# Gated feed-forward layers on one core: the down projection's pieces dealt among the products of each unit of seven

## The chip, the core and the metric

The kernel runs on one core of a Trainium2 chip. The metric is the device time of one execution in microseconds (us). TensorE does the matrix products, VectorE (DVE) most of the additions and subtractions, ScalarE (ACT) the roundings and copies, GpSimd (POOL) the sums of weights, and SyncE (SP) issues the transfers from the chip's memory. Each engine works through a queue of its own in the order in which the program was written, and waits at a semaphore where an operand is not yet made or a buffer not yet free.

## The reference

Two transformer blocks run one after the other on 512 tokens of width 1024. All weights and activations are float32. What matters here is the feed-forward part:

```
# first block, one layer
x = x + square(relu(rmsnorm(x, g) @ w_ff1)) @ w_ff2            # 1024 -> 4096 -> 1024

# second block, layers i = 0, 1
h = rms_norm(x, ffn_norm[i])
g = einsum('bsd,df->bsf', h, w_gate[i])                        # 1024 -> 2816
u = einsum('bsd,df->bsf', h, w_up[i])
x = x + einsum('bsf,fd->bsd', silu(g) * u, w_down[i])          # 2816 -> 1024
```

Three kinds of attention and their projections stand around it; the change does not touch them.

## The kernel before

Every float32 number is used as a rounded high part and the low part that is left over. A product of two such numbers takes three matmuls: high by high, high by low and low by high. In the trace a high part is `hh`, `wh` or `sums_high`, a low part `hl`, `wl` or `sums_low`; a low part is the subtraction at L2147, on DVE. Where a low part is written over its source the trace shows it under that name.

The kernel has three stages of feed-forward layers: stage 0 is the first block's (relu squared), stages 1 and 2 are the two gated layers of the second block. Most of their up and gate columns are computed in *units of seven* (class `Seven`): a product of 2 by 2 blocks with seven block products in place of eight. A unit of a gated stage yields two tiles of 128 features by 512 tokens, either of the gate or of the up matrix. The units alternate, gate, up, gate, up, sixteen in each gated stage. This is what one unit asks of each engine:

- **PE**: seven products P0 to P6, each of 12 matmuls of 128 columns by 256 tokens in three groups of four (L1343 high by high, L1346 with the tokens' low part, L1349 with the weights' low part).
- **DVE**: the low parts of the weights' seven operands (`wo_lo`, below lo0 to lo6, L2147), the additions that combine the products (`wc`, L2388, L2392 and L2397), and for the finished tiles a multiplication (`wf`, L2411: gate times sigmoid, or gate times up) and, for an up unit, the low part of the product that goes to the down projection (`wf_lo`, L2147, `R<-W,R`).
- **ACT**: the high parts of the operands, copies out of PSUM (L1897 and its neighbours), the sigmoid, and the high part of the finished tile (`wf_hi`, L1905).
- **POOL**: four sums of weights S1, S2, S4, S3 of the unit after the next (`ws`, L2769, four additions one behind the other).
- **SP**: the transfer of the weights of the unit after the next (`wq`, L2996). SP waits for the last low part (lo6) of a unit before it issues it, because the transfer lands in that unit's buffer.

Behind each unit of seven stands a *down unit*: 256 of the rows of `w_down` that belong to features finished earlier, or other rows of the same kind. It has four pieces d0 to d3, each of six matmuls 128 by 512 (L1265 twice, L1268 twice, L1271 twice), and each piece of it that ends is added to the residual `x` on DVE (L2438). The weights of the down units go through two buffers (raw, wh, wl): ACT rounds the high part (L1731), DVE makes the low part (`wl`, L2147), and a buffer is free when the last piece that reads it is done.

What sets the order of all this is the function `dense`. It makes a list of units and their pieces, moves some of them, and then goes through it: behind each piece it puts the steps for the other engines that the piece releases, and the steps that were put off (`defer`: so many pieces later). Each engine's queue is this list, cut to its own steps. The two lines that move pieces are L421 and L422 to L423; the second of them swaps P6 with the piece behind it, so that a unit runs P0 to P5, d0, P6, d1, d2, d3. `seven` names the steps of one product, with the distances of the final tiles' steps at L486 and L488 to L492. `preparation` puts the steps ahead of a stage at positions counted in pieces (sums of tokens `t_sum`, `t_hi`, `t_lo`, the first sums of weights `ws`), and `gated` inside `make` hands them to `dense`.

Of the kernel before, what the change touches and what calls it, by code (L numbers as in the profile page):

```python
# [196 lines left out]
SUMS_USED = (2, 0, 1, 3)  # L197
# [114 lines left out]
class Plan:  # L312
# [92 lines left out]
    def dense(self, units, more=None, crossed=False, hold=0, behind=False):  # L405

        n, order, held = 0, [], []  # L410
        for u in units:
            if u.kind == "win":
                pieces = [(k, 0, 0) for k in range(7)]
            elif u.kind == "rows":
                pieces = [(0, j * u.nk + k, j * u.nk + k + 2) for j in range(u.n) for k in range(0, u.nk, 2)]
            else:
                pieces = [(i, a, a + 2) for i in range(4) for a in range(0, 8, 2)]
            order += [(u, piece) for piece in pieces]
        if crossed:
            order = order[:3] + order[4:6] + order[3:4] + order[6:]  # L420
        for i in range(len(order) - 1, 0, -1):  # L421
            if order[i - 1][0].kind == "win" and order[i - 1][1][0] == 6:  # L422
                order[i - 1], order[i] = order[i], order[i - 1]  # L423
        for i, (u, piece) in enumerate(order):
            tick, extra = self.due() if behind else self.low() + self.due(), (more or {}).get(n, [])
            if behind:
                for step in self.low():
                    self.defer(1, *step)
            after = order[i + 1][0] if i + 1 < len(order) else u
            n += 1  # L430
            if u.kind == "win":
                yield [("wp", u, piece[0])], self.seven(u, piece[0]) + tick + extra
                continue
            self.place(u)
            if u.kind == "rows" and piece[2] % u.nk == 0:
                steps = self.ready(u, piece[2] // u.nk - 1)
                if u.ev == "out" and after.kind == "win" and after.stage and steps[0][0] == "split":
                    self.defer(2, *steps.pop(0))
                    self.defer(4, *self.lows.pop())
                if n <= hold:  # L440
                    held.append(steps.pop())
                    tick += steps + extra
                else:
                    self.gated(u)
                    tick += steps[:-1] + extra + steps[-1:]
            else:
                tick += extra
            if held and n > hold:
                tick.append(held.pop(0))
                self.gated(tick[-1][1])  # L450
            if u.halved(piece[1] // u.nk) and piece[2] % u.nk:
                tick += [("ev_half", u), ("ship_half", u)]
            if u.kind == "cols" and piece[2] == 8:
                if piece[0] == 3:
                    tick.append(("ev", u))
                    if u.ev == "dq":
                        self.heads(u)
                tick += self.split(u.chunks[piece[0]] + 2)
            yield [("mm", u, *piece)], tick
        rest = self.due(True)  # L460
        if rest:
            yield [], rest

    def seven(self, u, k):

        first, i = [], u.product(k)
        if k == 2:
            first.append(("wc", u, 1))
        if k == 5:
            first.append(("wcp", u, 3))  # L470
            self.defer(1, "wc", u, 2)
        if k in (1, 4):
            first.append(("wcp", u, {1: 1, 4: 2}[k]))
        if i + 3 < 7 * (u.last + 1):
            first.append(("wo_hi", i + 3))
        if i + 2 < 7 * (u.last + 1):
            first.append(("wo_lo", i + 2))
        if k == 6 and u.v + 2 <= u.last:
            first += [("wq", self.wins[u.v + 2]), ("ws", self.wins[u.v + 2])]
        if k == 6:  # L480
            self.defer(1, "wc", u, 3)
            if u.ev == "gate":
                self.defer(1, "wsig", u, 0)
                self.defer(2, "wsig", u, 1)
                self.defer(3, "wf", u, 0)
                self.defer(6, "wf", u, 1)  # L486
            else:
                late = u.stage and u.v < u.last  # L488
                for t in range(2):
                    self.defer((1, 6 if late else 2)[t], "wf", u, t)  # L490
                    self.defer((1, 7 if late else 2)[t], "wf_hi", u, t)
                    self.defer((2, 8 if late else 3)[t], "wf_lo", u, t)  # L492
        return first

    def preparation(self, v, stage, wins, tick):

        more, w = {}, wins[0].v
        last_up = self.last_up[stage]

        def put(n, *step):  # L500
            more.setdefault(n, []).append(step)

        put(tick + 3, "wq", wins[0])
        plain = stage == 0
        end = 32 if plain else 48
        for m in range(8):
            put(((13, 14, 16, 17, 18, 20, 21, 22) if plain else (14, 15, 17, 18, 20, 21, 23, 24))[m], "hn", v, stage, m)
        put(14, "ws", wins[0])
        for k in range(4):
            put(((22, 24, 25, 27) if plain else (26, 28, 30, 32))[k], "t_sum", stage, k)  # L510
            put(((24, 25, 27, 28) if plain else (28, 29, 31, 33))[k], "t_hi", stage, k)
            put(((28, 38, 49, 51) if plain else (34, 39, 57, 59))[k], "t_lo", stage, SUMS_USED[k])
        put(29, "wo_hi", 7 * w)
        put(31, "wo_lo", 7 * w)
        put(30, "wo_hi", 7 * w + 1)
        put(end + 10 if plain else end - 1, "wo_lo", 7 * w + 1)
        for i in range(3):
            put(end + i, "b_hi", stage, i, last_up)
            put(end + 2 + i, "b_lo", stage, i)
        put(end + (9 if plain else 10), "wq", wins[1])  # L520
        put(end + (9 if plain else 10), "ws", wins[1])
        put(end + 3, "wo_hi", 7 * w + 2)
        return more
# [2397 lines left out]
def sync_program(sp, S, B, plan, dram):  # L2921
# [65 lines left out]
    def seven(u):  # L2987
# [5 lines left out]
        else:  # L2993
# [3 lines left out]
            S[f"wq{u.v % 2}"], 16)  # L2997

    todo = {"wq": seven, "begin": begin, "split": split, "late": late, "c_turn": c_turn, "c_kt": c_kt, "again": again, "ship": ship, "ship_half": ship_half}
    for step in plan.steps:  # L3000
        if step[0] in todo:
# [85 lines left out]
```

## Time and profile before

| what | value |
|---|---|
| median of 3 runs | 2108.47 us (2108.09 to 2110.71) |
| the profiled execution's own time | 2110.2 us |
| its span in the trace | 2108.4 us |
| PE busy | 2092.7 us, 99% of the span |
| DVE busy | 1468.1 us, 70% |
| ACT busy | 1054.8 us, 50% |
| POOL busy | 407.6 us, 19% |
| granted clock of TensorE | 1.0 (the higher of its levels, 2.4 GHz) |
| the sixteen units of stage 1 | 1231.4 to 1476.3 us |
| the sixteen units of stage 2 | 1832.5 to 2079.6 us |

The span is what the trace covers, first instruction to last; the execution's own time is 1.8 us more. All times in the rows below are counted from the span's start. PE counts as busy from the start of a matmul to its modelled end, so neighbouring matmuls overlap: where PE runs without a break, the pace is the distance from start to start.

### The profile page before, as it was taken

The page shows a single profiled execution, that of the slowest core. Times are in us where ns is not written, and L with a number is a line of the kernel's source. Part 1 is how long each engine was busy: PE and PEld are TensorE (multiplying, and loading weights), DVE is VectorE, ACT ScalarE, POOL GpSimd, SP SyncE. Part 2 cuts the span into 40 slices and gives each one's busy share as a digit, 9 for nine tenths or more (in the row PEclk, how much of TensorE's full clock was granted, in tenths as well). Part 3 has the DMA queues.
Part 4 walks back from the last instruction along what each step waited for, and adds up shares of the span by engine and source line. Part 5 has one row for each costly group of instructions (what it writes and reads, how often), then busy time and mean ns, then how long its engine had stood idle before and what let it go on. Part 6 is the DMA issues. An engine that isn't in the chain of part 4 may idle for free.

```text
span 2108.4 us, 31641 instructions
## 1 busy us (share of the span) xinstructions
PE 2092.7 (99%) x12528; PEld 1731.9 (82%) x12528; DVE 1468.1 (70%) x2153; ACT 1054.8 (50%) x1798; POOL 407.6 (19%) x350
## 2 busy tenths in 40 slices
PE   9999999999999999999999999999999999999999
PEld 7768778778889898887777889999877667899998
DVE  5584774564587777664667888777657678888775
ACT  4463544554354343444455556555445565556553
POOL 0000432102012323010110133343011101143340
PEclk9999999999999999999999999999999999999999
DMA  4212112123242222122111332322221113232322
GB/s 173 80 61 84 58 55 95 48 64 129 90 140 87 114 91 110 62 95 84 51 61 62 118 111 91 121 91 90 80 90 60 60 41 110 91 120 91 119 102 70
DMA packets 45938, 187.18 MB, mean 89 GB/s; under 512 B 5216, under 2 KB 5728, under 8 KB 40032
## 3 DMA queue, kind: packets, MB, share of 16 engines
q1 hardware_dynamic: 45648, 184.98, 25.5%
q8 instruction: 100, 1.64, 0.3%
q14 instruction: 46, 0.38, 0.1%
q10 hardware_dynamic: 144, 0.18, 0.0%
HBM read 183.05 MB, written 2.10 MB: 88 GB/s over the span
## 4 chain that ended last, share of the span: by engine, by line
PE 93%; DVE 4%; ACT 1%; issue 1%; DMA 0%; SPq 0%; DVEq 0%; ACTq 0%
PE ps L1265 17%; PE ps L1268 16%; PE ps L1271 16%; PE ps L1346 7%; PE ps L1349 7%; PE ps L1343 7%; PE ps L1289 4%; PE ps L1292 4%; PE ps L1290 4%; PE ps L1244 3%; PE ps L1399 1%; PE ps L1451 1%; PE ps L1672 1%; PE ps L1654 1%; PE ps L1423 1%; PE ps L1469 1%
## 5 line engine op out<-in xcount | busy, mean ns | idle before, releaser
L1731 ACT CAST wh<-raw 128x1024 fp32r<-128x1024 f32 (+1 forms) x246 | 257.7, 1048 | 330.0 <-PE ps L1271 245.5
L2769 POOL TENSOR_TENSOR Q<-Q 128x512 f32<-128x512 f32 x176 | 268.8, 1527 | 775.3 <-DMA Q<-in_sevens 764.8
L2147 DVE TENSOR_TENSOR wl<-raw,wh 128x1024 fp32r<-128x1024 f32 (+2 forms) x250 | 308.4, 1234 | 151.8 <-ACT wh L1731 151.4
L1265 PE MATMUL ps<-R,wh 128*128 128x512 f32 x892 | 286.4, 402 | 0.2 <-DVE W L2326 0.2
L1268 PE MATMUL ps<-R,wl 128*128 128x512 f32 x892 | 276.9, 391 | 0.5 <-DVE wl L2147 0.5
L1271 PE MATMUL ps<-R,wh 128*128 128x512 f32 x892 | 276.1, 390 | 0.0
L1265 PE MATMUL ps<-hh,wh 128*128 128x512 f32 x704 | 231.2, 409 | 2.1 <-ACT wh L1737 0.9
L1268 PE MATMUL ps<-hh,wl 128*128 128x512 f32 x704 | 218.4, 391 | 0.6 <-DVE wl L2147 0.6
L1271 PE MATMUL ps<-hl,wh 128*128 128x512 f32 x704 | 217.5, 390 | 0.0
L1268 PEld LDWEIGHTS ps<-R,wl 128*128 128x128 f32 x892 | 167.2, 188 | 37.6 <-DVE wl L2147 1.4
L1271 PEld LDWEIGHTS ps<-R,wh 128*128 128x128 f32 x892 | 167.5, 188 | 36.1
L1265 PEld LDWEIGHTS ps<-R,wh 128*128 128x128 f32 x892 | 157.9, 189 | 35.2 <-issue 9.7
L2438 DVE TENSOR_TENSOR x<-ps,x 128x512 f32<-128x512 f32 x191 | 130.7, 688 | 77.9 <-PE ps L1271 75.3
L1265 PEld LDWEIGHTS ps<-hh,wh 128*128 128x128 f32 x704 | 125.4, 188 | 39.2 <-issue 15.1
L1268 PEld LDWEIGHTS ps<-hh,wl 128*128 128x128 f32 x704 | 131.8, 188 | 30.4 <-DVE wl L2147 2.1
L1271 PEld LDWEIGHTS ps<-hl,wh 128*128 128x128 f32 x704 | 132.2, 188 | 29.1 <-DVE hl L2228 0.3
L1289 PE MATMUL ps<-wh,hh 128*128 128x512 f32 (+1 forms) x384 | 155.0, 404 | 0.7 <-DVE F L2296 0.5
L2147 DVE TENSOR_TENSOR hl<-Q,hh 128x512 fp32r<-128x512 f32 (+1 forms) x163 | 143.5, 888 | 8.1 <-ACT hh L1857 8.1
L1292 PE MATMUL ps<-wh,hl 128*128 128x512 f32 (+1 forms) x384 | 148.7, 387 | 0.0
L1290 PE MATMUL ps<-wl,hh 128*128 128x512 f32 (+1 forms) x384 | 148.6, 387 | 0.0
L2147 DVE TENSOR_TENSOR wx<-Q,wx 128x512 fp32r<-128x512 f32 x154 | 132.9, 870 | 9.3 <-ACT wx L1857 9.3
L1905 ACT CAST R<-W 128x512 fp32r<-128x512 f32 x56 | 34.8, 622 | 151.7 <-DVE W L2403 81.9
(281 smaller groups left out, 3676.2 us busy)
## 6 DMA issues: line engine op xcount, KB each, us to landing
raw<-in_weights SPq DMA_DIRECT2D x244, 512.0 KB, 3.5
Q<-in_sevens SPq DMA_DIRECT2D x44, 1024.0 KB, 4.8
x<-in_x_t SPq DMA_DIRECT2D x4, 512.0 KB, 7.0
F<-in_x_t SPq DMA_DIRECT2D x4, 512.0 KB, 4.9
out<-x SPq DMA_DIRECT2D x7, 256.0 KB, 2.0
raw<-in_weights SPq DMA_DIRECT2D x4, 416.0 KB, 3.1
x<-in_bias SPq DMA_DIRECT2D x1, 1024.0 KB, 6.8
F<-in_weights SPq DMA_DIRECT2D x2, 384.0 KB, 3.8
```

Of the source, the lines that this page charges most:

```text
L1265: pe.matmul(out, hi[:, k, cs], B.tile(u.src, k)[0], start=k == 0, stop=False)
L1268: pe.matmul(out, lo[:, k, cs], B.tile(u.src, k)[0], start=False, stop=False)
L1271: last = pe.matmul(out, hi[:, k, cs], B.tile(u.src, k)[1], start=False, stop=k == u.nk - 1)
L1289: pe.matmul(out, B.hh[:, ts], hi[:, kk, :], start=k == 0, stop=False)
L1290: pe.matmul(out, B.hh[:, ts], lo[:, kk, :], start=False, stop=False)
L1292: last = pe.matmul(out, B.hl[:, ts], hi[:, kk, :], start=False, stop=k == 7)
L1343: pe.matmul(out, hi[:, n, :], high[:, n, :], start=n == 0 and k not in (4, 5, 6), stop=False, skip_group_check=True)
L1346: pe.matmul(out, hi[:, n, :], low[:, n, :], start=False, stop=False, skip_group_check=True)
L1349: last = pe.matmul(out, lo[:, n, :], high[:, n, :], start=False, stop=n == 3, skip_group_check=True)
L1731: act.copy(B.wh[s][:, 0:nk * ncol], B.raw[s][:, 0:nk * ncol]).then_inc(S["w_hi"], 1)
L2147: dve.tensor_tensor(lo, src, hi.bitcast(F32), ALU.subtract).then_inc(S[name], 1)
L2769: pool.tensor_tensor(B.weight_part(u.v, out), B.weight_part(u.v, a), B.weight_part(u.v, b), op).then_inc(S["w_s"], 1)
```

## The change

In the two gated stages the four pieces of the down unit are dealt among the products of the unit of seven ahead of it: P0, P1, d0, P2, P3, d1, P4, P5, d2, P6, d3. The swap of P6 and d0 is kept for stage 0 alone. The distances, in pieces, of the steps for the finished tiles are changed with it: the gate's second `wf` comes 5 pieces behind P6 in place of 6, and the up unit's second tile (`wf`, high part, low part) 2, 3 and 4 behind in place of 6, 7 and 8. In `preparation` the first sums of weights of a gated stage are put at position 42 in place of 14, and the last low part of the token sums at 58 in place of 59.

```diff
@@ dense
         if crossed:
             order = order[:3] + order[4:6] + order[3:4] + order[6:]
+        for i, (u, piece) in enumerate(order):
+            if u.kind == "win" and u.stage and piece[0] == 0:
+                order[i:i + 11] = [order[i + n] for n in (0, 1, 7, 2, 3, 8, 4, 5, 9, 6, 10)]
         for i in range(len(order) - 1, 0, -1):
-            if order[i - 1][0].kind == "win" and order[i - 1][1][0] == 6:
+            if order[i - 1][0].kind == "win" and order[i - 1][0].stage == 0 and order[i - 1][1][0] == 6:
                 order[i - 1], order[i] = order[i], order[i - 1]
@@ seven
-                self.defer(6, "wf", u, 1)
+                self.defer(5, "wf", u, 1)
             else:
                 late = u.stage and u.v < u.last
                 for t in range(2):
-                    self.defer((1, 6 if late else 2)[t], "wf", u, t)
-                    self.defer((1, 7 if late else 2)[t], "wf_hi", u, t)
-                    self.defer((2, 8 if late else 3)[t], "wf_lo", u, t)
+                    self.defer((1, 2)[t], "wf", u, t)
+                    self.defer((1, 3 if late else 2)[t], "wf_hi", u, t)
+                    self.defer((2, 4 if late else 3)[t], "wf_lo", u, t)
@@ preparation
-        put(14, "ws", wins[0])
+        put(14 if plain else 42, "ws", wins[0])
-            put(((28, 38, 49, 51) if plain else (34, 39, 57, 59))[k], "t_lo", stage, SUMS_USED[k])
+            put(((28, 38, 49, 51) if plain else (34, 39, 57, 58))[k], "t_lo", stage, SUMS_USED[k])
```

Three lines are added, so a line of the old kernel from L421 on stands three lines lower in the new one (L2147 is L2150 there). The queues of POOL and of SP are the same in both programs, instruction by instruction and wait by wait; those of PE, DVE and ACT differ.

On PE, in the first unit of seven of stage 1 (a gate unit), products are the rows with 128x256 and the down unit's pieces those with `R2` (the high tile), `R3` (its low part) and 128x512. Before, from the fifth product to the second piece:

```order
L1343 MATMUL ps<-sums_high,wx 128x256 x4
L1346 MATMUL ps<-sums_low,wx 128x256 x4
L1349 MATMUL ps<-sums_high,wx 128x256 x4
L1343 MATMUL ps<-hh,wx 128x256 x4
L1346 MATMUL ps<-hl,wx 128x256 x4
L1349 MATMUL ps<-hh,wx 128x256 x4
L1265 MATMUL ps<-R2,wh0 128x512 x2
L1268 MATMUL ps<-R2,wl0 128x512 x2
L1271 MATMUL ps<-R3,wh0 128x512 x2
L1343 MATMUL ps<-sums_high,hh 128x256 x4
L1346 MATMUL ps<-sums_low,hh 128x256 x4
L1349 MATMUL ps<-sums_high,hl 128x256 x4
```

After, in the same unit, from the fourth product to the third piece:

```order
L1346 MATMUL ps<-sums_high,hh 128x256 x4
L1349 MATMUL ps<-sums_low,hh 128x256 x4
L1352 MATMUL ps<-sums_high,hl 128x256 x4
L1268 MATMUL ps<-R2,wh0 128x512 x2
L1271 MATMUL ps<-R2,wl0 128x512 x2
L1274 MATMUL ps<-R3,wh0 128x512 x2
L1346 MATMUL ps<-sums_high,wx 128x256 x4
L1349 MATMUL ps<-sums_low,wx 128x256 x4
L1352 MATMUL ps<-sums_high,wx 128x256 x4
L1346 MATMUL ps<-hh,wx 128x256 x4
L1349 MATMUL ps<-hl,wx 128x256 x4
L1352 MATMUL ps<-hh,wx 128x256 x4
```

A piece stands now between each second product, and only one, d3, is left behind P6 where three were.

On DVE, where the first up unit of stage 1 ends and a gate unit begins: `W3<-ps,W3` is the last combination of the up unit, `W2` and `W3` its two tiles, `R1<-W2,R0` and `R1<-W3,R0` their low parts for the down projection, `hl<-Q0,hh` low parts of the next unit's weights (the first two here are lo2 and lo3), `W4<-ps,W4` the next unit's first combination, `x<-ps,x` a finished piece. Before:

```order
L2397 TENSOR_TENSOR W3<-ps,W3 128x512
L2411 TENSOR_TENSOR W2<-W2,W0 128x512
L2438 TENSOR_TENSOR x<-ps,x 128x512
L2147 TENSOR_TENSOR R1<-W2,R0 128x512
L2438 TENSOR_TENSOR x<-ps,x 128x512
L2147 TENSOR_TENSOR hl<-Q0,hh 128x4x128 x2
L2388 TENSOR_TENSOR W4<-ps,W4 128x256
L2147 TENSOR_TENSOR wx<-Q0,wx 128x512
L2411 TENSOR_TENSOR W3<-W3,W1 128x512
```

After:

```order
L2400 TENSOR_TENSOR W3<-ps,W3 128x512
L2414 TENSOR_TENSOR W2<-W2,W0 128x512
L2441 TENSOR_TENSOR x<-ps,x 128x512
L2150 TENSOR_TENSOR hl<-Q0,hh 128x4x128
L2150 TENSOR_TENSOR R1<-W2,R0 128x512
L2414 TENSOR_TENSOR W3<-W3,W1 128x512
L2150 TENSOR_TENSOR hl<-Q0,hh 128x4x128
L2150 TENSOR_TENSOR R1<-W3,R0 128x512
L2391 TENSOR_TENSOR W4<-ps,W4 128x256
```

Between the piece `x<-ps,x` and the second `hl` (lo3) stand now the first `hl`, a low part of a tile and a multiplication, where the two `hl` stood side by side before.

On DVE at the end of stage 1, behind the last unit of seven: `W6` and `W7` are its two tiles, `R3` their low parts, `wl1` the low part of the down weights for the second unit from there. Before:

```order
L2397 TENSOR_TENSOR W7<-ps,W7 128x512
L2411 TENSOR_TENSOR W6<-W6,W4 128x512
L2438 TENSOR_TENSOR x<-ps,x 128x512
L2147 TENSOR_TENSOR R3<-W6,R2 128x512
L2411 TENSOR_TENSOR W7<-W7,W5 128x512
L2147 TENSOR_TENSOR R3<-W7,R2 128x512
L2438 TENSOR_TENSOR x<-ps,x 128x512
L2147 TENSOR_TENSOR wl1<-raw1,wh1 128x1024
```

After:

```order
L2400 TENSOR_TENSOR W7<-ps,W7 128x512
L2414 TENSOR_TENSOR W6<-W6,W4 128x512
L2441 TENSOR_TENSOR x<-ps,x 128x512
L2150 TENSOR_TENSOR wl1<-raw1,wh1 128x1024
L2150 TENSOR_TENSOR R3<-W6,R2 128x512
L2414 TENSOR_TENSOR W7<-W7,W5 128x512
L2150 TENSOR_TENSOR R3<-W7,R2 128x512
```

The low part `wl1` of the down weights has moved ahead of the second tile's multiplication, which it stood behind.

## Rows read from the trace of the kernel before

**Rows 1.** The page: busy time by engine, and the load of one set of weights.

```profile
PE 2092.7 (99%) x12528; PEld 1731.9 (82%) x12528; DVE 1468.1 (70%) x2153; ACT 1054.8 (50%) x1798; POOL 407.6 (19%) x350
...
L1268 PEld LDWEIGHTS ps<-R,wl 128*128 128x128 f32 x892 | 167.2, 188 | 37.6 <-DVE wl L2147 1.4
```

**Rows 2.** Waits by line, 1800 to 2106 us: total us, times, longest; PE and PEld.

```profile
PE ps L1346 <- DVE sums_low L2147: 1.3, 1, 1.3
...
PEld ps L1343 <- ACT W L1897: 0.3, 1, 0.3
```

**Rows 3.** Windows, units of stages 1 and 2: us; busy PE, PEld, DVE, ACT, POOL; clock.

```profile
1231.40:1476.30 244.90, 244.90 (x1712) 229.87 (x1711) 190.86 (x253) 135.04 (x234) 98.40 (x68) 1.00 0.28 102
1832.50:2079.60 247.10, 245.71 (x1712) 230.07 (x1712) 196.21 (x252) 134.96 (x234) 89.16 (x60) 1.00 0.27 101
```

**Rows 4.** Timeline, PE, one up unit of stage 1: start, duration, engine, line, tiles.

```profile
1340.40 0.64 PE L1343 MATMUL ps<-hh,wx 128*128 128x256 f32 x4
...
1349.03 0.63 PE L1265 MATMUL ps<-R,wh 128*128 128x512 f32 x2
...
1350.42 0.64 PE L1343 MATMUL ps<-sums_high,hh 128*128 128x256 f32 x4
...
1351.85 0.63 PE L1265 MATMUL ps<-R,wh 128*128 128x512 f32 x2
...
1355.96 0.64 PE L1343 MATMUL ps<-hh,wx 128*128 128x256 f32 x4
```

**Rows 5.** Timeline, first unit of stage 2: DVE, POOL and PE.

```profile
1835.00 1.22 DVE L2147 TENSOR_TENSOR sums_low<-sums,sums_high 128x1024 fp32r<-128x1024 f32 x1
1842.09 2.30 DVE L2147 TENSOR_TENSOR sums_low<-sums,sums_high 128x1024 fp32r<-128x1024 f32 x1
...
1836.38 1.30 POOL L2769 TENSOR_TENSOR Q<-Q 128x512 f32<-128x512 f32 x1 [54.80 <-DMA Q<-in_sevens]
...
1844.44 0.74 PE L1346 MATMUL ps<-sums_low,hh 128*128 128x256 f32 x4 [1.25 <-DVE sums_low L2147]
```

**Rows 6.** Timeline, end of stage 1: PE, DVE and ACT.

```profile
1476.33 0.63 PE L1265 MATMUL ps<-R,wh 128*128 128x512 f32 x2
...
1480.43 0.62 PE L1265 MATMUL ps<-R,wh 128*128 128x512 f32 x2
...
1476.53 0.69 DVE L2397 TENSOR_TENSOR W<-ps,W 128x512 f32<-128x512 f32 x1 [2.33 <-PE ps L1349]
...
1479.12 0.69 DVE L2411 TENSOR_TENSOR W<-W 128x512 f32<-128x512 f32 x1
...
1481.72 1.23 DVE L2147 TENSOR_TENSOR wl<-raw,wh 128x1024 fp32r<-128x1024 f32 x1
...
1479.84 0.62 ACT L1905 CAST R<-W 128x512 fp32r<-128x512 f32 x1 [1.37 <-DVE W L2411]
1480.63 1.06 ACT L1731 CAST wh<-raw 128x1024 fp32r<-128x1024 f32 x1 [0.17 <-PE ps L1271]
```

**Rows 7.** Windows, the time behind stage 1; columns as in rows 3.

```profile
1476.30:1600.00 123.70, 123.70 (x567) 98.24 (x566) 71.13 (x105) 56.65 (x98) 10.95 (x12) 1.00 0.26 81
```

**Rows 8.** Timeline, behind the up unit of rows 4: two DVE subtractions beside POOL's sums.

```profile
1356.76 1.35 DVE L2147 TENSOR_TENSOR hl<-Q,hh 128x512 fp32r<-128x512 f32 x1
1358.04 1.78 DVE L2147 TENSOR_TENSOR hl<-Q,hh 128x512 fp32r<-128x512 f32 x1
...
1356.27 1.29 POOL L2769 TENSOR_TENSOR Q<-Q 128x512 f32<-128x512 f32 x1
1357.64 1.63 POOL L2769 TENSOR_TENSOR Q<-Q 128x512 f32<-128x512 f32 x1
```

**Rows 9.** Timeline, from a unit's last low part to POOL's next sums: DVE, SP's queue, POOL.

```profile
1363.01 0.68 DVE L2147 TENSOR_TENSOR hl<-Q,hh 128x512 fp32r<-128x512 f32 x1
...
1363.72 0.33 SPq L2996 DMA_DIRECT2D Q<-in_sevens  x1
...
1368.78 1.30 POOL L2769 TENSOR_TENSOR Q<-Q 128x512 f32<-128x512 f32 x1 [9.51 <-DMA Q<-in_sevens]
```

## Prediction

> **What bounds the kernel now.** I read the page first, then PE's waits, then the two gated stages as windows, and last the timeline at the places that the change touches. The page shows PE busy for 99% of the span [rows 1]: time can be won only where PE waits or runs slower than its matmuls need, and each new wait of PE is lost in full. The window of stage 1 is filled by PE to the last hundredth, 244.90 of 244.90 us. Stage 2 runs the same 1712 matmuls and takes 247.10 [rows 3]; the list of waits names what makes the difference: one wait of 1.3 us on the low part of a token sum and one of 0.3 us on a copy of ACT's [rows 2]. More than these 2.2 us the change cannot take away inside the units, since the granted clock is 1.00 throughout [rows 3]. Whether it brings new waits depends on two reserves: how late DVE finishes a low part before PE wants it, and how many down pieces lie between the last product of a unit and the next reader of its tiles.
>
> **The change part by part.** All times below are measured from starts of matmuls.
>
> *Border between products and pieces.* Six products take 1349.03 − 1340.40 = 8.63 us, the lone piece behind them 1350.42 − 1349.03 = 1.39, the lone product 1351.85 − 1350.42 = 1.43, and the three pieces 1355.96 − 1351.85 = 4.11 [rows 4]. So a run of n products costs 1.44n − 0.01, a run of n pieces 1.36n + 0.03: each pair of runs carries 0.02 us. A unit has two pairs of runs before and four after. 32 units × 2 × 0.02 = +1.3 us; bounds 0 and 2.6.
>
> The Trainium skill, page "TensorE: Matmul & The Clock Gate", section "Back-to-back issue gap", lets the distance between matmuls depend on their columns alone. By that rule the sum would be 1.3 us smaller; the lone piece at 1.39 us against 1.36 in a run speaks against it.
>
> *Waits that go.* In the first unit of stage 2, P6 waits for the second low part of the token sums. It stands before at 1842.09, behind subtractions that POOL's sums slow down from 1836.38 on; in the new order it follows directly on the one at 1835.00, ahead of POOL's start [rows 5]. PE then wants it eight us after it is made. This gives back at least the 1.3 + 0.3 of [rows 2] and at most the 2.2 of [rows 3], which holds the restarts too: −1.9 us. Earlier final tiles (distances 5 and 2, 3, 4) take nothing from PE's own queue.
>
> *First sums of weights at position 42.* POOL's queue and its waits are the same in both programs, and `ws` is a step of POOL alone. What starts these sums is the transfer, not the place in the list. Cost 0, with no other end to bound.
>
> *End of each gated stage.* Let P6 of the last unit end at 0 (1476.33). Before, three pieces follow, and the final down unit starts at 4.10 (1480.43) [rows 6]; its first piece reads tiles made earlier, its second one, 1.37 later at 5.47, the two of the last unit. After, only d3 follows: the final unit starts at 1.39, its second piece at 2.76, and the second matmul of that, 1.37/6 = 0.23 on, reads the second tile's high part at 2.99. When is that made? By the rows: combination at 0.20 (1476.53), then the first tile's multiplication. In the new order DVE then takes the finished piece (d3 is seen at 1.39 + 0.20 = 1.59) and, next, wl1. That waits for ACT's wh1, which in its turn waits for d3, the last reader of its buffer, as it did before (1480.63, 0.20 behind 1480.43). So wh1 runs from 1.59 to 2.65, wl1 starts at 2.68 and lets the next operation in after 1.23 − 0.08 = 1.15, at 3.83. Then the first tile's low part for 0.61, then the multiplication of the second tile, 4.44 to 5.13, then ACT's rounding 0.03 later for 0.62, to 5.78, and 0.05 to PE (the step from DVE's end at 1844.39 to PE's start at 1844.44 in [rows 5]): 5.83. PE waits 5.83 − 2.99 = 2.84 us; the first groups after a wait ran 0.74 in place of 0.64 [rows 4, 5], some 0.1 to 0.2 in all: 3.0. Before, that multiplication (1479.12) stood ahead of wl1 (1481.72) and the rounded tile was there at 1480.46, 4.13, with 1.3 us to spare. Two stages: +6.0 us, bounds 5.2 and 6.6.
>
> *From an up unit to the gate unit behind it.* There are seven such places in each stage, 14 in all. POOL makes its four sums when the transfer has landed; SP issues that when lo6 of the unit is done, and from lo6's end (1363.69) to POOL's start (1368.78) it took 5.09 us [rows 9]. Before, lo6 ended 1363.69 − 1355.96 = 7.73 into the unit, so POOL starts 2.74 us ahead of the next unit. After, lo6 stands behind the addition of the second piece d1, which ends at 2 × (2 × 1.44 − 0.01 + 1.39) = 8.52; with 0.20 of notice and two operations it ends at 10.0 at the earliest, by DVE's load nearer 10.5 of 15.6. POOL's window then begins between −0.5 and 0 of the gate unit; I take −0.1. It lies thereby over the four operations that DVE has to do there: lo2, the first tile's low part, the second tile's multiplication, lo3. Each takes two tiles that do not lie in PSUM. In [rows 8] such an operation ends 0.55 behind the POOL sum that it runs beside (1358.11 behind 1357.56; 1359.82 behind 1359.27), and the sum that follows takes 1.63 + 0.08 in place of 1.29 + 0.08. With the first sum's end at 1.25 and 1.71 for each of the others the four end at 1.8, 3.5, 5.2 and 6.9. PE wants lo3 in P3's last group: two products, a piece and a product are 5.69, and two groups of four matmuls are 0.96 more, 6.65, with the load of the weights 0.19 ahead [rows 1]: 6.46. It waits some 0.5, with the restart 0.6. Bounds: with POOL at −0.6 nothing; with POOL at +0.3 1.0; nearer to the row's own phase stands 0.6. 14 × 0.6 = +8.4 us, bounds 0 and 14. Before, lo2 and lo3 stood side by side behind the piece, at 0.80 and 2.08 of the unit (1356.76 and 1358.04), 2.6 us ahead of the reader. The transitions from gate to up hold fewer operations there, and I take them at 0.
>
> *Sum.* 1.3 − 1.9 + 6.0 + 8.4 = +13.8. On the profiled execution's 2110.2 us, 1.7 over the median, this gives 2124.0; for the median 2108.5 + 13.8 = 2122 us.
>
> **The rivals.**
>
> *B. lo3 is in time.* POOL's window begins early enough, or lo2 and the tile's low part slip in ahead of the first sum; then only the stage ends wait. For it: half a microsecond of POOL's phase decides, and DVE is busy for only 78% of the window of stage 1 (190.86 of 244.90) [rows 3]. Against it: all four operations wait for d3's addition or P6, which dealing has brought later against POOL. Time: 2108.5 + 1.3 − 1.9 + 6.0 = 2113.9.
>
> *C. Not slower: what PE loses at a stage's end it gets back behind it.* While PE stands for 3 us, DVE, ACT and the transfers go on; if PE would have to wait for one of these soon after, the later wait goes and nothing is lost. Decisive is whether such a wait of about 3 us lies behind each stage end and ahead of the next work that hangs on PE's own results. For it: ACT and DVE have the next weights to prepare there, and get ahead. Against it: PE is busy for 123.70 of 123.70 us behind stage 1 [rows 7]. With lo3 in time as well the sum would be 2108.5 + 1.3 − 1.9 = 2107.9 us.
>
> *D. POOL and DVE shut each other out.* By the rows a POOL sum beside a waiting DVE operation takes 1.63 us and DVE's ends 0.55 behind it, so the two run partly side by side. Were they to take turns in full, four sums and three DVE operations would stand one behind the other: 1.29 + 0.61 + 0.08 = 1.98 for each in place of 1.71, and lo3 would be 0.9 later (0.8 for the three periods, 0.1 for its own end). 14 × 0.9 = +12.6: 2135 us.
>
> The Trainium skill states this rule on the page "SBUF — State Buffer", section "SBUF: two separate sides": the pair of ports is an exclusive lock, and "whichever … starts first gets the pair for the whole instruction; the other fully blocks". The 0.55 of [rows 8], less than the 0.68 that the operation takes alone, does not bear it out in full.
>
> **How the numbers follow.** The forecast has 0.62 (its own range 2116 to 2129), B 0.24, C 0.05, D 0.04, and 0.05 is left for what I don't see. 0.2%, about what a measurement of this kernel can tell from no change, is 4.2 us. B lies at +5.4 with a spread of some 1.5 (border 0 to 2.6, ends 5.2 to 6.6), so a quarter of it, 0.06, falls under 4.2; C does wholly, and some 0.03 of the rest. Same: 0.06 + 0.05 + 0.03 = 0.14; faster 0.02, as PE's waits in the units hold no more than 2.2 us; slower 0.84. For eight in ten the range reaches from B's lower part, 2111, to where 1.1 us are lost at each transition, 2129.
>
> **What the changed profile would show.** Right: PE waits at the second piece of each final down unit for ACT's rounding of the second tile (L1908), 2.8 us each, with wl1 ahead of the multiplication on DVE; and at P3 of the gate units, in the group at L1352, for a low part of L2150, some ten to fourteen times. The window of each unit without a wait is 0.04 us longer. The wait for the token sum is gone. Wrong: no wait in the gate units, or one at another product; a piece that waits for its x or its wl; a POOL window that does not start close to the gate unit's start; or a stage end without a wait.

## The result, and the profile after

The changed kernel takes 2128.86 us (median of 4 runs, 2127.93 to 2130.46) against 2108.44: 1.0090 times as long, with a 95% interval of 1.0078 to 1.0102, or +20.4 us. Forecast were 2122 and a range of 2111 to 2129. The profiled execution took 2130.46 us, span 2128.7. All ratios compare runs in the faster of two states; one run of the kernel before, at 2283.99 us, is left out of them.

PE's list of waits over the whole span (total us, times, longest) has three lines that the kernel before did not have; the 1.3 us on `sums_low` of [rows 2] is gone.

```profile
PE ps L1268 <- ACT R L1908: 6.2, 2, 3.1
PE ps L1352 <- DVE wx L2150: 3.6, 8, 0.8
...
PE ps L1352 <- DVE hl L2150: 2.5, 6, 0.8
```

There are two waits at the second piece of a final down unit, one in each stage, and fourteen in the group of P3 that reads lo3 (its low part is called `wx` or `hl`, as the buffers alternate). These sum to 12.3 us, though, and the span grew by 20.3. The rest stands in the windows: the sixteen units from the first to the last product, and 5.8 us behind the wait at the end of stage 1 (columns as in [rows 3]).

```profile
1231.55:1485.13 253.58, 250.03 (x1722) 232.26 (x1721) 214.86 (x254) 134.94 (x234) 98.72 (x68) 1.00 0.27 98
1845.03:2097.41 252.38, 249.83 (x1722) 232.25 (x1721) 212.92 (x253) 134.81 (x234) 93.66 (x60) 1.00 0.27 99
1491.50:1497.30 5.80, 5.78 (x14) 4.53 (x15) 2.14 (x3) 1.24 (x2) 0.00 (x0) 0.50 0.15 62
```

The first two windows run over two pieces more than those of [rows 3], 2.7 us each, since only one piece of the last unit is left behind its P6. The last line tells what the list of waits does not: PE is busy there (5.78 of 5.80), but at a granted clock of 0.50, the lower of its two levels; before, it was 1.00 wherever the gated stages were looked at [rows 3, 7]. The timeline of PE at this place:

```profile
1488.01 0.39 PE L1268 MATMUL ps<-R,wh 128*128 128x512 f32 x1
1491.52 0.79 PE L1268 MATMUL ps<-R,wh 128*128 128x512 f32 x1 [3.12 <-ACT R L1908]
1492.11 1.05 PE L1271 MATMUL ps<-R,wl 128*128 128x512 f32 x2
...
1497.23 0.81 PE L1271 MATMUL ps<-R,wl 128*128 128x512 f32 x2
1497.88 0.62 PE L1274 MATMUL ps<-R,wh 128*128 128x512 f32 x2
```

Pairs that took 0.62 us take 1.05 for some six us behind the wait. If one adds up by how much the distances from matmul to matmul exceed 227 ns (128x512) and 120 ns (128x256), the two profiled executions compare as follows:

| term | forecast, us | stage 1 | stage 2 | together |
|---|---|---|---|---|
| fourteen waits at P3, with their restarts | +8.4 | 5.4 | 4.4 | +9.8 |
| a late low part at P5 of stage 1's first unit | 0 | 0.2 | 0 | +0.2 |
| stage ends: the wait | +6.0 (with restart) | 3.3 | 3.3 | +6.6 |
| stage ends: slower matmuls behind it | 0 | 2.9 | 1.7 | +4.6 |
| borders and other small distances | +1.3 | 0.5 | 0.6 | +1.1 |
| waits of stage 2 that are gone | −1.9 | 0 | −2.2 | −2.2 |
| sum | +13.8 | | | +20.1 of 20.3 |

The mechanism of the stage end, DVE and ACT from P6's end at 1485.26 on, answers to [rows 6]:

```profile
1486.85 0.69 DVE L2441 TENSOR_TENSOR x<-ps,x 128x512 f32<-128x512 f32 x1
1488.39 1.23 DVE L2150 TENSOR_TENSOR wl<-raw,wh 128x1024 fp32r<-128x1024 f32 x1 [0.85 <-ACT wh L1734]
1489.53 0.68 DVE L2150 TENSOR_TENSOR R<-W,R 128x512 fp32r<-128x512 f32 x1
1490.13 0.69 DVE L2414 TENSOR_TENSOR W<-W 128x512 f32<-128x512 f32 x1
...
1486.79 0.62 ACT L1908 CAST R<-W 128x512 fp32r<-128x512 f32 x1 [5.21 <-DVE W L2414]
1487.31 1.04 ACT L1734 CAST wh<-raw 128x1024 fp32r<-128x1024 f32 x1
1490.85 0.62 ACT L1908 CAST R<-W 128x512 fp32r<-128x512 f32 x1 [2.49 <-DVE W L2414]
```

wl waits for wh, the second multiplication stands behind wl, ACT's rounding behind that. It ends at 1491.47, 6.21 us behind P6 (forecast 5.78: ACT began wh late, at 2.05 in place of 1.59, since it was still rounding the first tile).

The mechanism at the gate units, DVE, POOL and PE at one that starts at 1359.35, answers to [rows 8]:

```profile
1359.55 0.69 DVE L2441 TENSOR_TENSOR x<-ps,x 128x512 f32<-128x512 f32 x1
1360.16 1.23 DVE L2150 TENSOR_TENSOR hl<-Q,hh 128x512 fp32r<-128x512 f32 x1
1361.32 1.78 DVE L2150 TENSOR_TENSOR R<-W,R 128x512 fp32r<-128x512 f32 x1
1363.02 1.77 DVE L2414 TENSOR_TENSOR W<-W 128x512 f32<-128x512 f32 x1
1364.72 1.78 DVE L2150 TENSOR_TENSOR hl<-Q,hh 128x512 fp32r<-128x512 f32 x1
...
1359.55 6.41 POOL L2772 TENSOR_TENSOR Q<-Q 128x512 f32<-128x512 f32 x4 [9.07 <-DMA Q<-in_sevens]
...
1366.55 0.62 PE L1352 MATMUL ps<-sums_high,hl 128*128 128x256 f32 x3 [0.39 <-DVE hl L2150]
```

What sets POOL's start is the up unit ahead, which starts at 1343.75: its lo6 (`hl`, L2150) ends at 1354.57, 10.8 us into it (forecast 10.0 to 10.5, before 7.7), and SP issues the transfer then.

```profile
1353.89 0.68 DVE L2150 TENSOR_TENSOR hl<-Q,hh 128x512 fp32r<-128x512 f32 x1
...
1354.59 0.33 SPq L2999 DMA_DIRECT2D Q<-in_sevens  x1
```

POOL's four sums begin 0.2 us into the gate unit; the four DVE operations behind `x` last 1.2 to 1.8 us each, and lo3 ends at 1366.50, 7.15 us into the unit (forecast 6.9).

### The profile page after: what moved, and what is told of

Read it like the earlier page. It is cut to its first block, busy times and chain, and to the rows that moved or that the text cites. A ratio compares the mean times of both kernels' runs of the same rounds, so it can differ in the third digit from the quotient of the medians.

```text
span 2128.7 us, 31641 instructions
## 1 busy us (share of the span) xinstructions
PE 2102.4 (99%) x12528; PEld 1735.5 (82%) x12528; DVE 1508.0 (71%) x2153; ACT 1054.4 (50%) x1798; POOL 411.7 (19%) x350
## 4 chain that ended last, share of the span: by engine, by line
PE 89%; DVE 8%; ACT 1%; issue 1%; DMA 0%; SPq 0%; DVEq 0%; ACTq 0%
PE ps L1268 16%; PE ps L1271 16%; PE ps L1274 16%; PE ps L1352 6%; PE ps L1349 6%; PE ps L1346 6%; PE ps L1292 4%; PE ps L1295 4%; PE ps L1293 4%; PE ps L1247 3%; PE ps L1402 1%; DVE R L2150 1%; DVE W L2414 1%; PE ps L1454 1%; DVE wx L2150 1%; PE ps L1675 1%
## 5 line engine op out<-in xcount | busy, mean ns | idle before, releaser
L2150 DVE TENSOR_TENSOR wl<-raw,wh 128x1024 fp32r<-128x1024 f32 (+2 forms) x250 | 311.8, 1247 | 154.1 <-ACT wh L1734 153.7
L1268 PE MATMUL ps<-R,wh 128*128 128x512 f32 x892 | 289.8, 405 | 6.5 <-ACT R L1908 6.2
L1268 PE MATMUL ps<-hh,wh 128*128 128x512 f32 x704 | 231.2, 409 | 1.8 <-DVE F L2288 0.7
L1268 PEld LDWEIGHTS ps<-R,wh 128*128 128x128 f32 x892 | 154.7, 190 | 37.4 <-issue 9.7
L1268 PEld LDWEIGHTS ps<-hh,wh 128*128 128x128 f32 x704 | 125.4, 188 | 38.8 <-issue 15.1
L2150 DVE TENSOR_TENSOR hl<-Q,hh 128x512 fp32r<-128x512 f32 (+1 forms) x163 | 144.0, 891 | 8.1 <-ACT hh L1860 8.1
L2150 DVE TENSOR_TENSOR wx<-Q,wx 128x512 fp32r<-128x512 f32 x154 | 136.6, 892 | 9.3 <-ACT wx L1860 9.3
L1908 ACT CAST R<-W 128x512 fp32r<-128x512 f32 x56 | 34.8, 621 | 187.4 <-DVE W L2414 105.8
```

What stands on the lines that cost most here:

```text
L1268: pe.matmul(out, hi[:, k, cs], B.tile(u.src, k)[0], start=k == 0, stop=False)
L2150: dve.tensor_tensor(lo, src, hi.bitcast(F32), ALU.subtract).then_inc(S[name], 1)
```

## The experiments

Theory: the time is lost at these two places, by the order of DVE's operations at the stage ends and by POOL's sums beside the four operations, and each can be taken away by itself. Rival: the dealing leaves DVE late in general, so that a wait that is removed comes back elsewhere.

### The last unit in the old order

```diff
-            if u.kind == "win" and u.stage and piece[0] == 0:
+            if u.kind == "win" and u.stage and piece[0] == 0 and u.v < u.last:
...
-            if order[i - 1][0].kind == "win" and order[i - 1][0].stage == 0 and order[i - 1][1][0] == 6:
+            if order[i - 1][0].kind == "win" and (order[i - 1][0].stage == 0 or order[i - 1][0].v == order[i - 1][0].last) and order[i - 1][1][0] == 6:
```

> The changed kernel, but the last unit of seven of each gated stage keeps the old order (three pieces behind P6). Theory: in the changed kernel each stage end costs a wait of 3.1 us for the second tile's high part, and behind it 13 matmuls at 427 ns in place of 227 (the granted clock is 0.51 there), 11 us for both ends. With three pieces behind P6 both go: about 2117.6 us, no wait for ACT's L1908, clock 1.00 throughout, and the 14 waits at P3 of the gate units stay (6 us in the list of waits). Rival: the stage end is late because of DVE's work left over from the dealt units; then the wait only moves to another piece and the time stays above 2125.

Measured: 2120.24 us (2119.73 to 2120.95) against 2108.09 before, ratio 1.0057 (1.0042 to 1.0072); about 2117.6 was expected. The waits at L1268 for L1908 are gone and the clock is 1.00. The waits at P3 stayed, and grew:

```profile
PE ps L1352 <- DVE wx L2150: 4.2, 8, 0.9
PE ps L1352 <- DVE hl L2150: 3.4, 6, 0.8
```

By the distances they cost 11.3 us here in place of 9.8, which is why the gain in the profiled executions is 9.5 us and not the 11.2 of the ends. The rival's wait at another piece did not come.

### The last unit dealt, but the tiles ahead of the down weights

```diff
+                ends = order[i - 1][0]
+                if ends.kind == "win" and ends.stage and ends.v == ends.last and steps[0][0] == "split":
+                    self.defer(2, *steps.pop(0))
+                    self.defer(3, *self.lows.pop())
...
-                    self.defer((1, 2)[t], "wf", u, t)
-                    self.defer((1, 3 if late else 2)[t], "wf_hi", u, t)
-                    self.defer((2, 4 if late else 3)[t], "wf_lo", u, t)
+                    self.defer((1, 1 if end else 2)[t], "wf", u, t)
+                    self.defer((1, 3 if late else 1 if end else 2)[t], "wf_hi", u, t)
+                    self.defer((2, 4 if late else 2 if end else 3)[t], "wf_lo", u, t)
```

Here `end` stands for the last unit of a gated stage.

> The changed kernel with the last unit dealt as well (one piece behind P6), but there DVE makes the second tile right behind the first, and the down weights' rounding and low part (wh1, wl1) come behind the tiles. Theory: the order on DVE and ACT is the cause, not the number of pieces: the second tile's high part is then made 2.75 us after P6, PE wants it at 2.99, the low part at 3.9 against 3.9: no wait of over 0.2 us, no lower clock, about 2117.7 us. Rival: one piece behind P6 is too little cover in any order; then a wait of over 1 us stays at the end of each stage and the time lies above 2120.

Measured: 2120.41 us (2119.99 to 2120.92), ratio 1.0057 (1.0042 to 1.0072), clock 1.00. In the distances, 0.16 us is left of the stage end at the first and 0.14 at the second. The time is 2.7 us above the 2117.7 expected, though no wait of 1 us stayed: that number took all of the ends' 11.2 us off the changed kernel's median, but 11.2 was the cost in its profiled execution, which took 1.6 us more than the median; the same two ends cost 10.0 us in the profile of the fourth experiment and 8.4 in that of the third. ACT rounds both tiles at once and then wh:

```profile
1486.90 1.23 ACT L1908 CAST R<-W 128x512 fp32r<-128x512 f32 x2 [5.21 <-DVE W L2414]
1488.03 1.05 ACT L1734 CAST wh<-raw 128x1024 fp32r<-128x1024 f32 x1
```

PE's order is that of the changed kernel, with one piece behind the last P6. So it is the place of wl and wh ahead of the second tile that made the end wait, and one piece is cover enough without it.

### lo3 ahead of the second tile

```diff
-                    self.defer((1, 2)[t], "wf", u, t)
-                    self.defer((1, 3 if late else 2)[t], "wf_hi", u, t)
-                    self.defer((2, 4 if late else 3)[t], "wf_lo", u, t)
+                    self.defer((1, 3 if late else 2)[t], "wf", u, t)
+                    self.defer((1, 4 if late else 2)[t], "wf_hi", u, t)
+                    self.defer((2, 5 if late else 3)[t], "wf_lo", u, t)
```

> The changed kernel with the up unit's second tile (multiplication, high part, low part) 3, 4 and 5 pieces behind P6 in place of 2, 3 and 4, so that lo3 stands ahead of that multiplication on DVE. Theory: lo3 is the third DVE operation beside POOL's sums in place of the fourth and ends 1.7 us earlier, 1.2 us before PE wants it: the 14 waits at L1352 (6.1 us with 0.1 of restart and some more each, 10.0 in the distances of the matmuls) go, about 2118.9 us; the stage ends stay at 3.1 us each. Rival: PE wants the next low part (lo4, pushed back in turn) too early as well, and the wait moves on by one product: above 2124.

Measured: 2126.59 us (2125.17 to 2127.87), ratio 1.0089 (1.0072 to 1.0106). The waits at L1352 are gone as expected, but the gain is 2.3 us in the medians, not 10: six new waits stand at a piece of the down unit, for the high part of the tile that was put off.

```profile
PE ps L1268 <- ACT R L1908: 10.9, 8, 3.1
```

Two of the eight are the stage ends, the others take 0.8 us each, 6.4 us in all by the distances:

```profile
1303.20 0.50 PE L1268 MATMUL ps<-R,wh 128*128 128x512 f32 x1 [0.78 <-ACT R L1908]
```

The rival holds here, though not with the low part that I named: the four operations take their time beside POOL, and whichever is last makes PE wait.

### POOL's sums later

```diff
     def weight_sums(u):
         at.wait_ge(f"wq{u.v % 2}", 16 * (u.v // 2 + 1))
+        if u.stage and u.ev == "up" and u.v - 2 >= u.others[0].v:
+            at.wait_ge("w_mm", plan.wins[u.v - 1].product(1) + 1)
```

> The changed kernel, but POOL waits with the four sums for an up unit until P1 of the gate unit ahead is done (3 us after the gate unit's start), so that they don't run beside lo2, the tile's low part, the second multiplication and lo3. Theory: without POOL beside them the four take 0.61 us each and lo3 ends at 3.3 us of the unit against 6.46 wanted: the waits at L1352 go though DVE's order is unchanged, about 2118.9 us, if POOL's later window does not delay another low part in the same way. Rival: DVE's order alone makes lo3 late, POOL has no part in it: all 14 waits stay, 2128.9 us.

Measured: 2119.89 us (2119.10 to 2120.52), ratio 1.0055 (1.0040 to 1.0070). All fourteen waits are gone from the list, with DVE's order unchanged. The timeline of DVE and POOL in a gate unit that starts at 1357.25:

```profile
1358.06 0.68 DVE L2150 TENSOR_TENSOR hl<-Q,hh 128x512 fp32r<-128x512 f32 x1
1358.66 0.68 DVE L2150 TENSOR_TENSOR R<-W,R 128x512 fp32r<-128x512 f32 x1
1359.26 0.69 DVE L2414 TENSOR_TENSOR W<-W 128x512 f32<-128x512 f32 x1
1359.87 0.69 DVE L2150 TENSOR_TENSOR hl<-Q,hh 128x512 fp32r<-128x512 f32 x1
...
1360.43 6.93 POOL L2774 TENSOR_TENSOR Q<-Q 128x512 f32<-128x512 f32 x4 [11.01 <-PE ps L1352]
```

The same four operations last 0.68 to 0.69 us each, and lo3 ends at 3.3 us of the unit where it ended at 7.15. This separates the two readings: DVE has time enough for them, and what it lost was lost to POOL.

### A shorter wait at the stage ends

As the second experiment, without its first four added lines: the second tile comes in time, but wl still stands ahead of both tiles' low parts.

```diff
-                    self.defer((1, 2)[t], "wf", u, t)
+                    self.defer((1, 1 if end else 2)[t], "wf", u, t)
...
+                    self.defer((1, 3 if late else 1 if end else 2)[t], "wf_hi", u, t)
...
+                    self.defer((2, 4 if late else 2 if end else 3)[t], "wf_lo", u, t)
```

> The changed kernel, but at the stage ends the second tile's multiplication stands right behind the first one's, while the down weights' low part still stands ahead of both tiles' low parts. The second tile's high part is then there in time, and PE should wait for the first tile's low part instead: wh1 ends at 3.84 us behind P6, wl1 at 5.0, the low part at 5.7, wanted at 3.67: 2.0 us of wait, in place of 3.1 to 3.3. Question: what the clock does behind a wait of that length. If it falls as behind the longer one, the two ends cost 2 x 2.0 + 4.6 and the time is about 2126.3; if it does not, 2 x 2.1 and about 2121.9.

Measured: 2127.57 us (2126.21 to 2128.83), ratio 1.0085 (1.0070 to 1.0099). PE waits for the low part as expected, 1.8 us in the list and 2.4 by the distances, with what follows at once; the windows behind the two waits differ:

```profile
PE ps L1274 <- DVE R L2150: 3.6, 2, 1.8
```

```profile
1490.70:1496.00 5.30, 5.20 (x21) 4.05 (x22) 2.97 (x5) 2.63 (x4) 0.00 (x0) 1.00 0.29 99
2101.70:2105.00 3.30, 3.30 (x9) 2.60 (x8) 0.00 (x0) 0.00 (x0) 0.00 (x0) 0.50 0.32 115
```

At the end of stage 1 the clock stayed at 1.00, at the end of stage 2 it fell to 0.50 behind a wait of the same length. So neither answer holds for each end (the median lies 1.3 us above the longer of the two times expected), and a wait of this length may or may not cost clock. Nor does the length alone decide with the longer wait, as the last section shows. What decides is not settled.

### Both places mended

The second and the fourth experiment's edits together; their core is:

```diff
+                    self.defer(2, *steps.pop(0))
+                    self.defer(3, *self.lows.pop())
...
+            at.wait_ge("w_mm", plan.wins[u.v - 1].product(1) + 1)
```

> The changed kernel with POOL's four sums put off to P1 of the gate unit and, at the stage ends, the tiles ahead of the down weights: both places that cost time are mended, the dealing itself stays. Theory: what is left of the change is the border cost (1.2 us in the distances of the matmuls) less the waits of stage 2 that it takes away (2.2 us), and 0.5 us of small waits seen in the two separate runs: 2107.5 to 2109 us, within 0.1% of the kernel before, no wait of over 0.2 us in the units. Rival: the two repairs disturb each other or dealing costs more than borders (the separate repairs gave back 8.4 and 9.0 us, of 20.4): 2111.5 or more.

Measured: 2110.01 us (2109.88 to 2110.85, 11 runs) against 2108.83, ratio 1.0001 (0.9992 to 1.0010). The list holds no wait of PE in the units of the two stages any more, and PE is busy throughout:

```profile
1232.34:1480.65 248.31, 248.31 (x1723) 231.93 (x1722) 216.28 (x254) 135.09 (x234) 101.95 (x68) 1.00 0.27 100
1834.57:2082.67 248.10, 248.10 (x1723) 231.90 (x1722) 215.58 (x253) 134.88 (x234) 99.00 (x60) 1.00 0.28 100
```

Dealing itself neither gains nor loses anything that this measurement can tell. (From first to last product a stage is 3.4 us longer than one without waits before because two pieces of the last unit, 2.7 us, now lie ahead of its P6; the rest are the borders.) The time is 1.0 to 2.5 us above what was expected, within the noise of the kernel before.

### The kernel before with the two edits of the preparation

```diff
-        put(14, "ws", wins[0])
+        put(14 if plain else 42, "ws", wins[0])
...
-            put(((28, 38, 49, 51) if plain else (34, 39, 57, 59))[k], "t_lo", stage, SUMS_USED[k])
+            put(((28, 38, 49, 51) if plain else (34, 39, 57, 58))[k], "t_lo", stage, SUMS_USED[k])
```

> The kernel before with the two edits of the preparation alone (positions 42 and 58; no dealing, old distances). By the order only one instruction moves: the second low part of the token sums on DVE, ahead of one subtraction and the down weights' low part. Theory: the wait of 1.3 us and its restart in the first unit of stage 2 goes, nothing else changes: 1.5 to 2 us less, 2106.3 to 2106.8. Rival: the subtraction and wl, now 2.3 us later beside POOL's sums, are late in turn: no gain or up to 1 us more, 2108 to 2109.

Measured: 2108.07 us (2107.96 to 2110.57, 11 runs) against 2108.83, ratio 0.9997 (0.9987 to 1.0006): no difference that can be told, where 1.5 to 2 us less were expected. The wait is gone from this profiled execution, but the edit cannot be credited with it, as the rows in the last section show. No version tried is clearly faster than the kernel before.

## Why the prediction was right, and where its sizes were off

- *Border between products and pieces.* +1.3 forecast, +1.1 found in the distances.
- *First sums of weights at position 42.* No wait of PE came of it; in the changed kernel, too, POOL's first sums of both stages start by the transfer.
- *From an up unit to the gate unit.* Fourteen waits forecast in P3's last group, fourteen found, +9.8 for +8.4. lo6 ended 0.3 us later than forecast, and POOL began 0.2 us into the gate unit where I took −0.1. The fourth experiment shows the cause. One reading was wrong, though no term hangs on it: the reserve of 2.6 us for lo3 in the kernel before was counted to the place that its reader has in the new order. In the old one P3's last group stands at 1361.23 and lo3 ends at 1359.82, which leaves 1.2 us ahead of the load of its weights.
- *End of each gated stage.* The place, the chain and the instruction were as forecast, the wait 3.3 us by the distances for 2.84. The term was mis-sized all the same, +11.2 for +6.0 and far over its bound of 6.6: I priced PE's standstill and a restart of 0.2, and left out that the clock can fall behind it. That cost 2.9 and 1.7 us in this execution, 1.7 and 1.7 behind the same waits in the fourth experiment's, and 1.7 and 0.1 in the third's. No row of before showed a lower clock, and no wait of PE in that kernel's list is longer than 1.4 us.
- *Waits that go.* −2.2 in the profiled execution for −1.9. Most runs of the kernel before seem to be without this wait: twenty of the times on record lie at 2107.8 to 2108.9 and eleven at 2109.4 to 2113.9, and the profile with the wait took 2110.2. No trace of a run without it was kept, and the last experiment's kernel has two such levels too (nine of eleven runs at 2108.0 to 2108.4, two at 2110.5). If it is so, the forecast took away from the median what only its one profile had.
- *Rivals.* B (lo3 in time) fell by the list of waits. So did C (made good later): between the two stages the lists of both kernels hold the same waits of the same length, so nothing was given back. D (full turns, lo3 0.9 us later) would have cost +12.6 us more; the fourteen waits took 0.7 us each, near the 0.6 forecast. More on its rule stands below.
- *The number.* 2128.86 lies just inside the range's end of 2129, 6.9 us above the forecast. That end stood for 1.1 us at each gate unit; the gate units took 0.7, and most of what filled the range up was the clock behind the stage ends, which had no price. The places and the chains were forecast; that the range held was luck.

## What to carry to other kernels

When work is dealt more evenly on the engine that bounds, look at what used to stand last: three pieces behind the last product were the cover for a chain of four operations on other queues, and an operation that waits for a freed buffer must not stand ahead of the ones that feed the bounding engine. When an order on one engine shifts a trigger, follow it to every engine that it starts: here lo6 came later, the transfer with it, and POOL's sums fell on DVE's four urgent operations. A long wait of PE can cost slow matmuls behind it as well: here 0 to 2.9 us behind a wait of some 3 us.

## What the hardware showed that was not expected

*The clock behind a wait.* Three profiles have a standstill of 3.3 us at both stage ends: those of the changed kernel, of the third and of the fourth experiment. Behind five of the six TensorE ran at a granted clock of 0.50 for some three to six us (427 ns for a 128x512 matmul in place of 227). Behind the sixth, at the end of stage 2 in the third experiment, the clock stayed at 1.00:

```profile
2100.16 0.50 PE L1268 MATMUL ps<-R,wh 128*128 128x512 f32 x1 [3.12 <-ACT R L1908]
```

```profile
2100.20:2106.00 5.80, 5.80 (x26) 4.79 (x27) 2.58 (x4) 1.06 (x1) 0.00 (x0) 1.00 0.29 106
```

Behind 2.0 us it fell at one stage end and not at the other.

*Who comes first, POOL or DVE.* In the kernel before POOL's first sum of stage 1 began with a DVE subtraction already at work (by 0.01 us), and this is how both went on, DVE and POOL:

```profile
1235.94 1.28 DVE L2147 TENSOR_TENSOR wx<-Q,wx 128x512 fp32r<-128x512 f32 x2
1237.14 1.22 DVE L2147 TENSOR_TENSOR wl<-raw,wh 128x1024 fp32r<-128x1024 f32 x1
1238.28 1.22 DVE L2147 TENSOR_TENSOR sums_low<-sums,sums_high 128x1024 fp32r<-128x1024 f32 x1
...
1235.95 5.92 POOL L2769 TENSOR_TENSOR Q<-Q 128x512 f32<-128x512 f32 x1 [56.26 <-DMA Q<-in_sevens]
```

DVE's subtractions keep their pace and POOL's one sum lasts 5.92 us in place of 1.30. In stage 2 of the same execution POOL came first (1836.38, while DVE read PSUM) and DVE was slowed, its second sum lasting 2.30 in place of 1.22 [rows 5]: that is the wait of P6. In the last experiment's stage 2 DVE's subtraction started no later than POOL's sum:

```profile
1836.88 0.68 DVE L2147 TENSOR_TENSOR wx<-Q,wx 128x512 fp32r<-128x512 f32 x1
...
1836.88 5.91 POOL L2769 TENSOR_TENSOR Q<-Q 128x512 f32<-128x512 f32 x1 [54.94 <-DMA Q<-in_sevens]
```

So there the wait would probably be gone by that alone, and the experiment does not tell the edit from the luck of the start. These rows agree with the rule of the Trainium skill ("SBUF — State Buffer", section "SBUF: two separate sides"), that who starts first has the shared ports to itself for its whole instruction, better than the prediction allowed: 5.92 us in place of 1.30 for POOL's sum. The rule speaks of one instruction; that DVE's next ones kept POOL out as well is what these rows add. Only D's sum from the rule was wrong: taking turns does not cost both durations in full, but 1.71 us a turn, which the row of before had shown.
